# First RMS norm: factor per token applied behind the input projection, x transposed as it lands, first slab in two halves by rows

## The chip, the cores and the metric

The kernel runs on one core of one Trainium2 chip. The metric is the device time of one execution in microseconds. Each profile is of one such execution.

## The reference

Two transformer blocks on 256 tokens of width 1024, in float32. What bears on the change is the head of the first block:

```
xn = x * rsqrt(mean(x * x, axis=-1) + EPS) * attn_norm_g      # one factor per token, one gain per feature
proj = xn @ w_in                                              # mq, mk, mv (softmax attention), gq, gk, gv, gr, gate_lr (gated linear attention)
mq, mk = rope(mq), rope(mk)                                   # cos and sin per token and feature
log_a = log_sigmoid(gate_lr @ w_gate_up + b_gate) / 16
og = gla_attention(gq, gk, gv, log_a)                         # chunked, G = cumsum(log_a)
y_gla = rms_norm(og) * gla_norm_g * silu(gr)
```

After it follow the output projection, a feed-forward with a short convolution, and the second block, which the change leaves alone.

## The kernel before, in words

Every engine has its own program, written out by hand, and engines wait for each other on semaphores. All weights come as 117 slabs of 128 x 2048 floats (1 MB), in the order of the list `STREAM`, through three buffers `raw`. For each slab ScalarE (ACT) writes the rounded high part `hiw` (L616, helper `rnd`) and VectorE (DVE) the rest, `low` = raw - hiw (L1059, helper `res`); both have three buffers too. TensorE (PE) then makes three products per tile of 128 x 128: high by high, high by low, low by high (`three`, L1702 to L1704), 48 of 256 columns for a slab of the input projection. SyncE (SP) issues the next slab when `low` of the slab three before it is made.

The start: PE multiplies zeros `WARM` = 12 times (`keep_clock`, L1634) while x comes in. ACT squares token tile 0 and half of tile 1 (`first_squares`), DVE the other half; the factor of each token comes out of a logarithm and an exponential. DVE multiplies the rows of x by it (L1072), PE turns the 16 tiles (`first_turn`, L1647), ACT makes the high part `xhi` with the gain per feature (L645), DVE the rest `xlo` (L1080). Then PE computes `gg`, the small product for the gates, with `smh` and `sml`; two more products of zeros; the slab `gq` in two halves by columns; `z`, the gates' second product (L1835); the slab `gk`; and then the slabs mq0, mk0, mv0, mq1, mk1, mv1, gv0, gv1, gr0, gr1. Behind slab k stand the score products of the gated attention, one level of block size L after another (`level`; L1862 for most, L1859 for L = 128). The levels 0 and 128 both come behind mq0.

GpSimd (POOL) prepares the levels. It starts on two events, and for the first two levels does four differences and two scalings of 128 x 256, with an exponential of ACT between them:

```
pool.wait_ge(*given_back("gk"))
pool.wait_ge(s("gates_summed"), 1)
for i, L in enumerate(GLA_LEVELS[1:]):
    ...
    pool.tensor_tensor(late, g_late, mid, ALU.subtract)
    pool.tensor_tensor(early, mid, g_early, ALU.subtract).then_inc(s("level_diff"), 1)
    if i:
        scale_level(i - 1)
```

`given_back("gk")` is the moment at which the slab's product has been copied out of PSUM; `gates_summed` comes from DVE's running sums (L1187). PE's level 128 waits for the first `scale_level` (L559, L560), in line with everything behind it. `tok`, `gg`, `z` and so on are leases of PSUM banks: `full` is PE's signal, `given_back` the reader's.

## Time and profile before

| | |
|---|---|
| time, median of 3 runs | 737.99 us (737.91 to 738.71) |
| the profiled execution | 737.9 us, of which the span of the trace is 736.1 us |
| PE busy | 720.2 us (98%) |
| DVE busy, ACT busy, POOL busy | 546.8 us (74%), 380.1 us (52%), 57.2 us (8%) |
| DMA | 129.27 MB, mean 176 GB/s |

Busy shares are means over the whole span. What bounds a stretch is read from who waits in it: from the chain of waits, followed back from the last instruction, and from the timeline.

### The profile page before, as it was taken

The numbers are of one execution on the slowest core, as the hardware profiler recorded it, in microseconds if no ns is written. First come the engines' busy times: TensorE is split into PE (matmuls) and PEld (weight loads), VectorE is DVE, ScalarE is ACT, GpSimd is POOL, SyncE is SP. The second block draws the span as 40 slices with busy tenths as digits, with TensorE's granted clock in tenths as the row PEclk, the third lists the DMA queues.
The fourth block names the chain that finished last, engine by engine and source line by source line (L and its number), as shares of the span: only waits on it lengthen the run. The fifth ranks groups of instructions, "written<-read, shape, count | busy, mean of one in ns | idle before, by whom it ended". The sixth has DMA issues, their size and how long they took to land.

```text
span 736.1 us, 11503 instructions
## 1 busy us (share of the span) xinstructions
PE 720.2 (98%) x4488; PEld 637.9 (87%) x4488; DVE 546.8 (74%) x645; ACT 380.1 (52%) x471; POOL 57.2 (8%) x64
## 2 busy tenths in 40 slices
PE   8999999999999999989999999999999999999998
PEld 8999887888888888778989888999888888888886
DVE  6679847889998889966558857787788666656663
ACT  7635466766555555555564543544457344344341
POOL 1455100000330000011000000000000000000000
PEclk9999999999999999999999999999999999999999
DMA  9835333165555555333543444445535655455431
GB/s 361 321 131 202 115 115 145 71 228 206 209 177 212 181 177 211 127 115 132 215 155 134 168 172 172 172 172 202 198 115 179 222 190 210 171 187 212 173 115 57
DMA packets 18954, 129.27 MB, mean 176 GB/s; under 512 B 2272, under 2 KB 2528, under 8 KB 3680
## 3 DMA queue, kind: packets, MB, share of 16 engines
q1 hardware_dynamic: 18912, 128.68, 48.0%
q8 instruction: 30, 0.49, 0.3%
q14 instruction: 12, 0.10, 0.0%
HBM read 126.57 MB, written 1.05 MB: 173 GB/s over the span
## 4 chain that ended last, share of the span: by engine, by line
PE 90%; DVE 6%; ACT 2%; issue 1%; POOL 0%; DVEq 0%; POOLq 0%; ACTq 0%
PE ps L1726 20%; PE ps L1702 13%; PE ps L1703 13%; PE ps L1704 13%; PE ps L1734 10%; PE ps L1746 7%; PE ps L1748 4%; DVE low L1059 2%; ACT hiw L616 1%; PE ps L1862 1%; PE ps L1634 1%; PE ps L1674 1%; PE ps L1682 1%; PE ps L1675 1%; PE ps L1659 1%
## 5 line engine op out<-in xcount | busy, mean ns | idle before, releaser
L616 ACT ACTIVATE hiw<-raw 128x2048 fp32r<-128x2048 f32 x116 | 222.0, 1915 | 205.8 <-PE ps L1734 97.6
L1059 DVE TENSOR_TENSOR low<-raw,hiw 128x2048 fp32r<-128x2048 f32 x116 | 267.9, 2313 | 80.2 <-ACT hiw L616 79.6
L1726 PE MATMUL ps<-xx,hiw 128*128 128x512 f32 x672 | 159.9, 390 | 0.0
L1726 PEld LDWEIGHTS ps<-xx,hiw 128*128 128x128 f32 x672 | 124.5, 188 | 24.8
L1734 PEld LDWEIGHTS ps<-xx,low 128*128 128x128 f32 x672 | 86.0, 191 | 3.1
L1734 PE MATMUL ps<-xx,low 128*128 128x256 f32 x672 | 87.3, 283 | 0.0
L1702 PE MATMUL ps<-hiw,yhi 128*128 128x512 f32 x208 | 81.7, 393 | 2.0 <-DVE ylo L1363 1.5
L1703 PE MATMUL ps<-low,yhi 128*128 128x512 f32 x208 | 81.2, 390 | 0.0
L1704 PE MATMUL ps<-hiw,ylo 128*128 128x512 f32 x208 | 81.0, 389 | 0.0
L1318 DVE TENSOR_REDUCE arena<-ps 128x512 f32<-128x1024 f32 x42 | 51.3, 1221 | 24.1 <-PE ps L1734 24.0
L1746 PE MATMUL ps<-xx,hiw 128*128 128x512 f32 x256 | 64.8, 395 | 0.9 <-DVE arena L1537 0.9
L1702 PE MATMUL ps<-xx,hiw 128*128 128x256 f32 x224 | 64.3, 287 | 1.0 <-DVE low L1059 1.0
L1703 PE MATMUL ps<-xx,hiw 128*128 128x256 f32 x224 | 63.3, 283 | 0.0
L1704 PE MATMUL ps<-xx,low 128*128 128x256 f32 x224 | 63.3, 283 | 0.0
L1746 PEld LDWEIGHTS ps<-xx,hiw 128*128 128x128 f32 x256 | 46.1, 189 | 10.1 <-DVE arena L1537 1.1
L1702 PEld LDWEIGHTS ps<-hiw,yhi 128*128 128x128 f32 x208 | 39.1, 188 | 10.6 <-DVE ylo L1363 1.9
L1704 PEld LDWEIGHTS ps<-hiw,ylo 128*128 128x128 f32 x208 | 39.1, 188 | 8.3
L1703 PEld LDWEIGHTS ps<-low,yhi 128*128 128x128 f32 x208 | 39.1, 188 | 7.3
L1336 DVE SCALAR_TENSOR_TENSOR arena<-arena,vec 128x255 f32<-128x255 f32 x88 | 40.5, 481 | 5.8 <-ACT arena L863 1.5
L1702 PEld LDWEIGHTS ps<-xx,hiw 128*128 128x128 f32 x224 | 42.9, 192 | 2.0 <-issue 1.7
L1703 PEld LDWEIGHTS ps<-xx,hiw 128*128 128x128 f32 x224 | 42.9, 192 | 0.0
L1704 PEld LDWEIGHTS ps<-xx,low 128*128 128x128 f32 x224 | 42.9, 192 | 0.0
(239 smaller groups left out, 1023.1 us busy)
## 6 DMA issues: line engine op xcount, KB each, us to landing
raw<-in_slabs SPq DMA_DIRECT2D x117, 1024.0 KB, 4.8
vec<-in_vec SPq DMA_DIRECT2D x1, 1258.5 KB, 9.0
cst<-in_cst SPq DMA_DIRECT2D x1, 1220.0 KB, 13.3
h<-in_x SPq DMA_DIRECT2D x2, 512.0 KB, 3.7
arena<-arena SPq DMA_DIRECT2D x16, 64.0 KB, 2.8
out<-h SPq DMA_DIRECT2D x1, 512.0 KB, 2.7
out<-h SPq DMA_DIRECT2D x2, 256.0 KB, 2.0
vec<-in_vec SPq DMA_DIRECT2D x1, 229.0 KB, 4.8
```

What stands on the lines that cost most here:

```text
L616: act.activation(hiw[:, n % SPLIT, :], raw[:, n % RAW, :], ACT.Copy).then_inc(hi_made, 1)
L1059: dve.tensor_tensor(low[:, n % SPLIT, :], raw[:, n % RAW, :], hiw[:, n % SPLIT, :].bitcast(F32), ALU.subtract).then_inc(lo_made, 1)
L1318: dve.tensor_reduce((hid if k == "ffn1" else up)[par][j], wide_hidden(j).rearrange("p c (a b) -> p c b a", a=2), AX_X, ALU.add).then_inc(h ...
L1336: ins = dve.scalar_tensor_tensor(out=dst[:, o:], in0=src[:, 0:T - o], scalar=w, in1=dst[:, o:], op0=ALU.mult, op1=ALU.add)
L1634: pe.matmul(bank(name)[:, 0:P], zeros[:, :], zeros[:, :], start=True, stop=True)
L1702: pe.matmul(o, whi, mhi, start=start, stop=False)
L1703: pe.matmul(o, whi, mlo, start=False, stop=False)
L1704: return pe.matmul(o, wlo, mhi, start=False, stop=stop)
L1726: pe.matmul(banks[:, c, :], hi[:, kt, cc_], xx[:, kt].rearrange("p a b -> p (a b)"), start=kt == 0, stop=False)
L1734: mm = pe.matmul(banks[:, c, 0:T], lo[:, kt, cc_], xhi[:, kt, :], start=False, stop=kt == KT - 1)
L1746: pe.matmul(o, hi[:, kt, cc_], xx[:, kt].rearrange("p a b -> p (a b)"), start=kt == 0, stop=False)
L1748: mm = pe.matmul(o[:, 0:T], lo[:, kt, cc_], xhi[:, kt, :], start=False, stop=kt == KT - 1)
```

## The change

The rows of x are no longer scaled. PE turns x itself, tile 0 as soon as it and the identity have landed, then tile 1. `xhi` and `xlo` hold x times the gain alone. Everything computed from them lacks the factor of its token, which is multiplied in later: where tokens lie on partitions (mv0, mv1, gv0, gv1) by ACT as it copies out of PSUM; where tokens lie in columns (gg, gq, gk, gr0, gr1) by DVE with a tile `token_scale`, which holds the factors along the columns and is made by two small products (`spread_tokens`) inside the slab gq; for mq and mk in the tables of cosine and sine. ACT squares tile 0 first and tile 1 only behind the first slab's rounding. The first slab comes as two transfers, by rows (contraction tiles 0 to 3, then 4 to 7). PE does all its products with the high part first, then `spread_tokens`, then those with the low part; gk goes the same way. The vectors' first part comes in two transfers, the constants' first part ahead of x's tile 1. The warm-up has 8 products of zeros in place of 12, and the two ahead of gq are gone.

```diff
-WARM = 12
+WARM = 8
...
-            for tt in range(TT):
-                sp.dma_start(h[:, tt, :], x_in[tt * P:(tt + 1) * P, :]).then_inc(s(f"x{tt}_in"), 16)
+            sp.dma_start(h[:, 0, :], x_in[0:P, :]).then_inc(s("x0_in"), 16)
             sp.dma_start(cst[:, 0:C_FIRST], cst_in[:, 0:C_FIRST]).then_inc(s("cst_first_in"), 16)
-            sp.dma_start(vec[:, 0:V_FIRST], vec_in[:, 0:V_FIRST]).then_inc(s("vec_first_in"), 16)
-            sp.dma_start(raw[:, 0, :], slabs_in[0]).then_inc(raw_full[0], 16)
+            sp.dma_start(h[:, 1, :], x_in[P:T, :]).then_inc(s("x1_in"), 16)
+            sp.dma_start(vec[:, 0:V_GAINS], vec_in[:, 0:V_GAINS]).then_inc(s("vec_gains_in"), 16)
+            sp.dma_start(row_half(raw[:, 0, :], 0), row_half(slabs_in[0], 0)).then_inc(s("half_in"), 16)
+            sp.dma_start(row_half(raw[:, 0, :], 1), row_half(slabs_in[0], 1)).then_inc(raw_full[0], 16)
+            sp.dma_start(vec[:, V_GAINS:V_FIRST], vec_in[:, V_GAINS:V_FIRST]).then_inc(s("vec_first_in"), 16)
...
-            act.wait_ge(*full("gg"))
-            act.activation(ggT[0:GATE_RANK, :], bank("gg")[0:GATE_RANK, 0:T], ACT.Copy).then_inc(*frees("gg"))
-            evacuate("gq", gqT, scale=SCALE)
+            act.wait_ge(s("vec_first_in"), 16)
             act.wait_ge(*full("z"))
...
             rnd(3)
-            evacuate("gk", gkT)
             rnd(4)
...
-                evacuate(name, DST[name])
+                if name[1] == "v":
+                    act.wait_ge(*full(name))
+                    for tt in range(TT):
+                        ins = act.activation(DST[name][:, tt, :], bank(name)[:, tt * 256:(tt + 1) * 256], ACT.Copy,
+                                             scale=norm_scale(0, tt))
+                    ins.then_inc(*frees(name))
+                elif name[1] != "r":
+                    evacuate(name, DST[name])
...
+            def times_tokens(name, dst, scale=1.0):
+
+                dve.wait_ge(*full(name))
+                n = token_scale.unsqueeze(1).broadcast_to([P, 2, T])
+                dve.scalar_tensor_tensor(out=dst, in0=two(name), scalar=scale, in1=n, op0=ALU.mult,
+                                         op1=ALU.mult).then_inc(*frees(name))
...
+            dve.wait_ge(s("rstd_made"), TT)
+            for tt in range(TT):
+                dve.tensor_scalar(spread[:, tt, :], onesT[:, 0:P], norm_scale(0, tt), None, ALU.mult)\
+                   .then_inc(s("spread_made"), 1)
+            dve.wait_ge(*full("tok"))
+            dve.tensor_copy(token_scale, bank("tok")[:, 0:T]).then_inc(*frees("tok"))
+            dve.wait_ge(*given_back("tok"))
+            dve.wait_ge(*full("gg"))
+            dve.tensor_tensor(ggT[0:GATE_RANK, :], bank("gg")[0:GATE_RANK, 0:T], token_scale[0:GATE_RANK, :],
+                              ALU.mult).then_inc(*frees("gg"))
             res(1)
+            times_tokens("gq", gqT, SCALE)
             res(2)
...
             last.then_inc(s("gates_summed"), 1)
+            times_tokens("gk", gkT)
             res(3)
             dve.wait_ge(s("cst_rest_in"), 16)
             me.step(dve, dve.tensor_reduce(st[:, 34:35], C(C_ROT), AX_X, ALU.add))
-            me.step(dve, dve.tensor_scalar(sin_signed, C(C_SIN, T), st[:, 34:35], -1.0, ALU.mult, ALU.mult))
+            dve.scalar_tensor_tensor(out=sin_signed, in0=C(C_SIN, T), scalar=st[:, 34:35], in1=token_scale,
+                                     op0=ALU.mult, op1=ALU.mult)
+            me.step(dve, dve.tensor_tensor(C(C_COS, T), C(C_COS, T), token_scale, ALU.mult))
...
+                if k >= 10:
+                    times_tokens(IN1[k], grT[:, 2 * (k - 10):2 * (k - 10) + 2, :])
...
                 for tt in range(TT):
+                    pe.wait_ge(s(f"x{tt}_in"), 16)
                     for kt in range(KT):
-                        if kt % 4 == 0:
-                            pe.wait_ge(s("rows_scaled"), 2 * tt + kt // 4 + 1)
                         o = bank(f"n0_{kt // 2}")[:, kt % 2 * T + tt * P:kt % 2 * T + (tt + 1) * P]
-                        mm = pe.transpose(o, hn[0][:, tt, kt * P:(kt + 1) * P], ident)
+                        mm = pe.transpose(o, h[:, tt, kt * P:(kt + 1) * P], ident)
...
+            def first_slab(o, n):
+
                 hi, lo = slab_views(n, KT)
+                for half, high_made in enumerate(((s("half_hi"), 1), (hi_made, 1))):
+                    pe.wait_ge(*high_made)
+                    for c in range(2):
+                        for kt in range(half * KT // 2, (half + 1) * KT // 2):
+                            for m in (xhi, xlo):
+                                pe.matmul(o[:, c * T:(c + 1) * T], hi[:, kt, c * P:(c + 1) * P], m[:, kt, :],
+                                          start=half == 0 and c == 0 and kt == 0 and m is xhi, stop=False)
+                spread_tokens()
...
             take_bank(pe, "gq")
-            keep_clock("gq", 2)
-            pe.wait_ge(s("half_lo"), 1)
-            feature_half(bank("gq"), AT[("in1", "gq")], 0)
-            pe.wait_ge(lo_made, 1)
-            feature_half(bank("gq"), AT[("in1", "gq")], 1).then_inc(*fills("gq"))
+            first_slab(bank("gq"), AT[("in1", "gq")]).then_inc(*fills("gq"))
```

**The order on PE at the start.** Before, the 16 turns (L1647) stand behind 12 products of zeros and behind the scaled rows (`rows_scaled`, DVE's L1072):

```order
L1634 MATMUL ps<-zeros 128x128 [waits zeros_made]
L1634 MATMUL ps<-zeros 128x128 x11
L1647 MATMUL ps<-cst,arena 128x128 [waits rows_scaled,cst_first_in]
L1647 MATMUL ps<-cst,arena 128x128 x3
L1647 MATMUL ps<-cst,arena 128x128 [waits rows_scaled]
```

Of the change, where the turns are L1657, the products of gq L1784 (high) and L1791 (low), and the two small products L1800:

```order
L1645 MATMUL ps<-zeros 128x128 x7
L1657 MATMUL ps<-cst,h 128x128 [waits x0_in,cst_first_in]
L1657 MATMUL ps<-cst,h 128x128 x7
L1657 MATMUL ps<-cst,h 128x128 [waits x1_in]
```

```order
L1784 MATMUL ps<-xx,hiw 128x256 [waits half_hi]
L1784 MATMUL ps<-xx,hiw 128x256 x15
L1784 MATMUL ps<-xx,hiw 128x256 [waits hi_made]
L1784 MATMUL ps<-xx,hiw 128x256 x15
L1800 MATMUL ps<-cst,arena 128x128 [waits spread_made] x2
L1791 MATMUL ps<-xx,low 128x256 [waits half_lo]
```

The turns wait for transfers alone, and the two small products stand between the high and the low products of the first slab.

**The order on DVE from the gates' running sums to the slab mq0.** Before (L1187 are the sums, L1059 the low parts of slabs 3 and 4, L1192 the sine table):

```order
L1187 SCALAR_TENSOR_TENSOR arena<-arena 128x256
L1059 TENSOR_TENSOR low<-raw,hiw 128x2048 [waits hi_made]
L1191 TENSOR_REDUCE st<-cst 128x1 [waits cst_rest_in]
L1192 TENSOR_SCALAR arena<-cst,st 128x256 [waits dve_step]
L1059 TENSOR_TENSOR low<-raw,hiw 128x2048 [waits hi_made,dve_step]
```

Of the change (L1159 is `times_tokens` of gk, waiting for PE's bank; L1199 and L1201 are the sine and the cosine table):

```order
L1193 SCALAR_TENSOR_TENSOR arena<-arena 128x256
L1159 SCALAR_TENSOR_TENSOR arena<-ps,arena 128x512 [waits bank_full1]
L1059 TENSOR_TENSOR low<-raw,hiw 128x2048 [waits hi_made]
L1198 TENSOR_REDUCE st<-cst 128x1 [waits cst_rest_in]
L1199 SCALAR_TENSOR_TENSOR arena<-cst,st,arena 128x256 [waits dve_step]
L1201 TENSOR_TENSOR cst<-cst,arena 128x256
L1059 TENSOR_TENSOR low<-raw,hiw 128x2048 [waits hi_made,dve_step]
```

Copying gk out of PSUM has moved from ACT to DVE, ahead of the low part of slab 3, and one more instruction stands between the low parts of slabs 3 and 4.

## Rows read from the trace of the kernel before

**Rows 1.** The page: the chain that ended last, share of the span by engine.
```profile
PE 90%; DVE 6%; ACT 2%; issue 1%; POOL 0%; DVEq 0%; POOLq 0%; ACTq 0%
```

**Rows 2.** The chain of waits, 0 to 10 us: start, length, what.
```profile
0.98 5.49 PE ps L1634 x24
...
8.00 0.85 ACT xx L645 x2
```

**Rows 3.** Timeline to 27 us: start us, us, engine line op out<-in [idle before <-releaser].
```profile
4.06 1.06 ACT L625 ACTIVATE arena<-h 128x1024 f32<-128x1024 f32 x1 [2.05 <-DMA h<-in_x]
...
5.29 0.69 DVE L1066 CUSTOM_DVE_ANT_0 arena<-h 128x512 f32<-128x512 f32 x1 [5.29 <-DMA h<-in_x]
...
10.87 2.06 ACT L692 ACTIVATE hiw<-raw 128x1024 fp32r<-128x1024 f32 x2
...
19.27 1.13 PE L1835 MATMUL ps<-arena,vec 16*128 16x256 f32 x4
...
26.38 0.60 ACT L680 ACTIVATE arena<-ps 128x512 f32<-128x512 f32 x1 [1.30 <-PE ps L1704]
```

**Rows 4.** Lines L1634 (to 6.5 us, and at 13 us) and L1647: ns min/median/max.
```profile
L1634 PE MATMUL ps<-zeros x21: 421/421/421, 1.8 to 6.1; 128*128 128x128 f32 x21
...
L1634 PE MATMUL ps<-zeros x3: 271/274/275, 13.0 to 13.2; 128*128 128x128 f32 x3
...
L1647 PE MATMUL ps<-cst,arena x9: 272/273/329, 7.3 to 8.3; 128*128 128x128 f32 x9
```

**Rows 5.** SP's issues, and DMA issues to 20 us (KB each, median us to landing).
```profile
1.64 0.43 SPq L490 DMA_DIRECT2D cst<-in_cst  x1
2.11 0.43 SPq L491 DMA_DIRECT2D vec<-in_vec  x1
...
vec<-in_vec SPq DMA_DIRECT2D x1, 229.0 KB, 4.8
cst<-in_cst SPq DMA_DIRECT2D x1, 66.0 KB, 4.1
```

**Rows 6.** Timeline of DVE and POOL, 25 to 35 us.
```profile
25.22 2.27 DVE L1059 TENSOR_TENSOR low<-raw,hiw 128x2048 fp32r<-128x2048 f32 x1
...
27.72 0.39 DVE L1192 TENSOR_SCALAR arena<-cst,st 128x256 f32<-128x256 f32 x1
28.88 2.43 DVE L1059 TENSOR_TENSOR low<-raw,hiw 128x2048 fp32r<-128x2048 f32 x1 [0.77 <-ACT hiw L616]
33.22 1.29 DVE L1202 TENSOR_TENSOR arena<-ps,cst 128x512 f32<-128x512 f32 x2 [1.91 <-PE ps L1862]
...
27.05 0.91 POOL L577 TENSOR_TENSOR arena<-arena 128x256 f32<-128x256 f32 x1 [23.94 <-ACT arena L680]
...
28.55 0.62 POOL L577 TENSOR_TENSOR arena<-arena 128x256 f32<-128x256 f32 x1
29.13 2.66 POOL L578 TENSOR_TENSOR arena<-arena 128x256 f32<-128x256 f32 x1
31.75 0.73 POOL L559 TENSOR_TENSOR arena<-arena 128x256 f32<-128x256 f32 x1
32.44 0.73 POOL L560 TENSOR_TENSOR arena<-arena 128x256 f32<-128x256 f32 x1
```

**Rows 7.** Level 128 on PE: its row, and its wait (total us, times, longest).
```profile
33.22 0.72 PE L1859 MATMUL ps<-arena 64*128 64x128 f32 x8
...
PEld ps L1859 <- POOL arena L560: 0.2, 1, 0.2
```

**Rows 8.** Timeline of DVE and POOL, 43 to 48 us.
```profile
43.95 1.18 POOL L560 TENSOR_TENSOR arena<-arena 128x256 f32<-128x256 f32 x1
...
44.45 2.82 DVE L1059 TENSOR_TENSOR low<-raw,hiw 128x2048 fp32r<-128x2048 f32 x1
```

**Rows 9.** PE's waits over the whole span, the longest single one.
```profile
PE ps L1885 <- DVE arena L1245: 1.6, 1, 1.6
```

**Rows 10.** Timeline of DVE near slab gr0.
```profile
100.46 2.29 DVE L1059 TENSOR_TENSOR low<-raw,hiw 128x2048 fp32r<-128x2048 f32 x1 [6.12 <-ACT hiw L616]
```

More of the change, by code:

```diff
@@ L92 @@
 V_W = _at
+V_GAINS = V_LAY["small"][1]
 V_FIRST = V_LAY["wup"][1]
@@ L402, in build @@
         ggT = piece(5120, 256)
+        spread, token_scale = piece(12288, TT, P), piece(4608, T)
         gqT, gkT, G = (piece(5376 + 512 * j, 2, T) for j in range(3))
@@ L466, in pv_done, with row_half @@
             return full(f"mo{hh // 2}" if hh < 8 else f"fo{(hh - 8) // 2}")
-        def column_half(t, c):
-            return t.rearrange("p (k c) -> p k c", k=KT)[:, :, c * P:(c + 1) * P]
+        def row_half(t, half):
+            return t[:, half * SLAB // 2:(half + 1) * SLAB // 2]
         def level_halves(t, i):
@@ L682, in _ @@
             tables("natural_log_exp_and_others")
[L683 to L688 removed]
+            first_sum(0)
+            act.wait_ge(s("vec_gains_in"), 16)
             first_turned()
+            act.wait_ge(s("half_in"), 16)
+            act.activation(row_half(hiw[:, 0, :], 0), row_half(raw[:, 0, :], 0), ACT.Copy).then_inc(s("half_hi"), 1)
             act.wait_ge(raw_full[0], 16)
[L691 to L693 removed]
+            act.activation(row_half(hiw[:, 0, :], 1), row_half(raw[:, 0, :], 1), ACT.Copy).then_inc(hi_made, 1)
+            first_sum(1)
             rnd(1)
             rnd(2)
[L697 to L699 removed]
+            act.wait_ge(s("vec_first_in"), 16)
             act.wait_ge(*full("z"))
@@ L766, in _ @@
             DST = {"mq0": qpre[0], "mk0": qpre[1], "mq1": qpre[0], "mk1": qpre[1], "mv0": mv[:, :, 0, :],
-                   "mv1": mv[:, :, 1, :], "gv0": gv[:, :, 0, :], "gv1": gv[:, :, 1, :], "gr0": grT[:, 0:2, :],
-                   "gr1": grT[:, 2:4, :]}
+                   "mv1": mv[:, :, 1, :], "gv0": gv[:, :, 0, :], "gv1": gv[:, :, 1, :]}
             ropes = 0
@@ L1172, in _ @@
             first_turned()
-            dve.wait_ge(s("half_hi"), 1)
-            dve.tensor_tensor(column_half(low[:, 0, :], 0), column_half(raw[:, 0, :], 0),
-                              column_half(hiw[:, 0, :], 0).bitcast(F32), ALU.subtract).then_inc(s("half_lo"), 1)
-            dve.wait_ge(hi_made, 1)
-            dve.tensor_tensor(column_half(low[:, 0, :], 1), column_half(raw[:, 0, :], 1),
-                              column_half(hiw[:, 0, :], 1).bitcast(F32), ALU.subtract).then_inc(lo_made, 1)
-            dve.memset(onesT, 1.0).then_inc(s("ones_made"), 1)
+            for half, (high, low_half) in enumerate((((s("half_hi"), 1), (s("half_lo"), 1)), ((hi_made, 1), (lo_made, 1)))):
+                dve.wait_ge(*high)
+                dve.tensor_tensor(row_half(low[:, 0, :], half), row_half(raw[:, 0, :], half),
+                                  row_half(hiw[:, 0, :], half).bitcast(F32), ALU.subtract).then_inc(*low_half)
+            dve.wait_ge(s("ones_made"), 1)
+            dve.wait_ge(s("rstd_made"), TT)
[8 more added lines that the diff above has]
+                              ALU.mult).then_inc(*frees("gg"))
             res(1)
+            times_tokens("gq", gqT, SCALE)
             res(2)
             dve.wait_ge(s("z_ln"), 1)
-            dve.wait_ge(s("ones_made"), 1)
             me.step(dve, dve.scalar_tensor_tensor(out=zb, in0=zb, scalar=0.0, in1=za, op0=ALU.min, op1=ALU.subtract))
@@ L1764, in feature_major_late, with spread_tokens @@
                 return mm
-            def feature_half(o, n, c):
+            def first_slab(o, n):
                 hi, lo = slab_views(n, KT)
-                cc_ = slice(c * P, (c + 1) * P)
-                for kt in range(KT):
-                    mm = three(o[:, c * T:(c + 1) * T], hi[:, kt, cc_], lo[:, kt, cc_], xhi[:, kt, :], xlo[:, kt, :],
-                               kt == 0, kt == KT - 1)
-                return mm
+                for half, high_made in enumerate(((s("half_hi"), 1), (hi_made, 1))):
[6 more added lines that the diff above has]
+                spread_tokens()
+                for half, low_made in enumerate(((s("half_lo"), 1), (lo_made, 1))):
+                    pe.wait_ge(*low_made)
+                    for c in range(2):
+                        for kt in range(half * KT // 2, (half + 1) * KT // 2):
+                            mm = pe.matmul(o[:, c * T:(c + 1) * T], lo[:, kt, c * P:(c + 1) * P], xhi[:, kt, :],
+                                           start=False, stop=half == 1 and c == 1 and kt == KT - 1)
+                return mm
+            def spread_tokens():
+                take_bank(pe, "tok")
+                for tt in range(TT):
+                    pe.wait_ge(s("spread_made"), tt + 1)
+                    mm = pe.matmul(bank("tok")[:, tt * P:(tt + 1) * P], spread[:, tt, :], ident, start=True, stop=True)
+                mm.then_inc(*fills("tok"))
             def token_major(o, n, middle=None):
```

52 lines of the change are left out of this document (17 added, 35 removed).

## The prediction

> **What bounds the kernel now.** I read the chain of waits first. PE holds 90% of it, DVE 6%, ACT 2% [rows 1]: PE runs nearly without a gap, so a microsecond counts only if it moves PE's next instruction. Then I read the chain's first 10 us. The reader is to see that PE's products of zeros carry it to about 6.5 us, and that `xhi` starts at 8.0 [rows 2]; everything on PE hangs on that start. The timeline gives the fixed points behind it: the first slab's rounding at 10.87, `z` on PE at 19.27, and the copy of gk out of PSUM at 26.38, which says that PE ended gk at 26.35 [rows 3]. Last I read the two engines that are not in the chain, DVE and POOL, around the first levels [rows 6], because the change reorders DVE exactly there. PE reached level 128 at 33.2 and waited 0.2 us for POOL's L560 [rows 7]. That small wait is the hinge of this forecast: POOL's preparation of level 128 was already level with PE.
>
> **The start, step by step.** Removed: the scaling of the rows (DVE, L1072) and the wait for both factors. The new gate for the turns is landing plus warm-up. The 24 halves of 12 products of zeros took 5.49 us [rows 2], or 0.22 to 0.23 us each, so 16 of them end at 0.98 + 3.6 = 4.6 us. x's tile 0 had landed when ACT started at 4.06, tile 1 when DVE started at 5.29 [rows 3]. The constants, queued behind both, landed at 1.64 + 4.1 = 5.7, and the vectors at 2.11 + 4.8 = 6.9 [rows 5]. In the new order the constants go second. I take 4.5 for them (0.45 behind x's tile 0, as they were behind tile 1), 5.7 for tile 1 (the same bytes as before the constants' old landing), and 6.3 for the gains (half of the vectors' old 1.2 us). The bounds for the constants are 4.1 and 5.7.
>
> The turns then run from 4.6. PE's clock matters here. The products of zeros took 421 ns each until 6.1 us and 271 to 275 ns at 13 us, and the turns from 6.5 us on took 272 ns [rows 4]: PE was at 1.2 GHz for the whole warm-up and at 2.4 GHz behind it, having multiplied without a stop since 0.98. Nine turns begin between 7.3 and 8.3, so one costs about 0.11 us at the high level [rows 4], and I take twice that, 0.21, at the low one. Eight turns of tile 0 end at 6.3, two of tile 1 are out by 6.5 to 6.6, and the result is there 0.2 to 0.3 us later: `xhi` starts at 6.8 in place of 8.0. **The lead is 1.2 us.** It is at most 1.7, when PE is at the high level from the start of the turns and the gains' landing at 6.3 is the gate; it is at least 0.5, when the constants land at 5.7 and tile 0 is turned after that.
>
> Between `xhi` and `z` the changed steps balance. From `z` at 19.27 to gk's copy at 26.38 PE did `z` (1.1 us) and 48 products [rows 3], some 0.12 us each; counted back, 48 of them and 0.4 us for two products of zeros put the end of gg at 12.9 before and 11.7 now. ACT's rounding of the first slab keeps its distance of 2.87 us from `xhi` (8.00 to 10.87 [rows 2, 3]), so the halves are rounded at 10.8 and 11.8; PE needs the first at 11.7 and the second, 16 products on, at 13.6. The two products of zeros ahead of gq go, and `spread_tokens` brings two of the same shape: nothing. The factors: ACT squares tile 1 behind the rounding (1.06 us for tile 0 [rows 3], and under 1 us for logarithm and exponential), is done by 13.7, and PE asks for the spread at 15.5. ACT's rounding of slab 1 is 0.5 us later than before and PE asks for it at 19.1. Those costs are all nothing as long as PE is that late; if the cover went, each would cost its excess alone. So `z` starts at 18.1, and gk ends at 26.4 - 1.2 = 25.2.
>
> Later additions: mv and gv leave PSUM in two instructions instead of one (some 0.15 us more of ACT, which waits for PE's banks around them), gr0 and gr1 move to DVE, which was idle 6.1 us there [rows 10]. Nothing.
>
> **What the lead runs into.** POOL may start on the levels when gk is out of PSUM. Before, from 26.4 on: DVE's low part of slab 3 had begun at 25.22, so POOL's first difference at 27.05 was held only for its tail (0.91 us where an undisturbed one takes 0.62). The low part of slab 4 then started at 28.88, and POOL's fourth difference took 2.66 us, 2.05 more than its own length; when DVE was done, POOL went on with L559 at 31.75 and L560 at 32.44, each about 0.7 [rows 6]. It holds the other way too: the low part took 2.82 us beside POOL's L560, which took 1.18, against 2.27 alone [rows 6, 8]. So the two engines exclude each other in such instructions, and take turns.
>
> Of the change, DVE has to wait for gk before it makes the low part of slab 3, since `times_tokens` of gk now stands ahead. POOL is released by that same copy, while DVE goes straight on into the low part. POOL now meets the whole of it and not its tail. From the end of gk, in us:
>
> - copy of gk on DVE, half of the pair of equal size at 33.22 [rows 6]: 0.65
> - low part of slab 3, POOL held: 2.1
> - four differences of POOL: 2.4
> - the sine and the cosine table, two inputs from SBUF each, where the sine had one (0.39 us, which held nobody): 0.3 each, 0.6
> - low part of slab 4, which is ready before the fourth difference: 2.1
> - the two scalings: 1.4
>
> That is 9.25 us, so L560 ends at 25.2 + 9.25 = 34.45, where before it ended at 33.17. PE would reach level 128 at 33.2 - 1.2 = 32.0 and stands 2.5 us. Level 128 starts 1.25 us later than before. If the two tables hold nobody, it is 8.65 us and 0.65 later. ACT's exponential and its rounding of slab 4 (1.9 us from 25.2) lie inside. Queued behind level 128 on PE is everything: mk0, level 64, the other slabs. On ACT the exponential for the next level, the copy of mq0 and the rounding of slab 5 stand behind POOL's fourth difference, so they move with PE's delay. I find no wait on PE after this that ends at a transfer or at another event not itself set off by PE, so the 1.25 us reach the end.
>
> **The rule that speaks against the change.** The Trainium skill, page "SBUF — State Buffer", section "Who interferes with whom", says that a VectorE instruction with two SBUF inputs and a GpSimd instruction that reads SBUF hold a shared port for the whole of each instruction. By that rule both tables belong in the list, which gives the larger sum, 739.15; without the rule the rows leave 738.55 open. The 2.66 us of [rows 6] agree with it.
>
> **The sum.** The profiled execution took 737.9 us, its span 736.1, so 1.8 lie around it; it is 0.1 under the median of the runs, 737.99. 737.9 + 1.25 = 739.15. I forecast 739.1 us.
>
> **The rivals.**
>
> 1. *The lead survives*: POOL gets through between DVE's instructions. If it does its four differences in one go after the low part of slab 3, L560 ends at 25.2 + 0.65 + 2.1 + 2.4 + 1.4 = 31.75, ahead of PE's 32.0, and the time is 737.9 - 1.2 = 736.7 (736.2 to 737.4 over the lead's bounds). For it: DVE pauses between reduction and tables, and the low part of slab 4 might come late. Against it: at 28.88 DVE came up while POOL was in its third difference, and DVE went first [rows 6]. A milder form, in which one of the low parts falls outside POOL's work, gives 25.2 + 7.15 = 32.35, 0.85 earlier than before: 737.05.
>
> 2. *The start gains nothing, and the stall comes all the same*: slower. The place is the turns; the price is the lead. If the constants land at 5.7 or PE is still at 1.2 GHz when gg begins, the lead is 0, gk ends at 26.4 and L560 at 35.65, which makes 740.35. It decides from a lead under 0.9, where the end passes 0.2% over the median. For it: with 8 products of zeros there is a possible gap before the turns, which was none before. Against it: the turns take the place of the zeros, so PE multiplies on from 4.6 to about 7.5. The Trainium skill, page "TensorE: Matmul & The Clock Gate", section "What's actually happening", says that the moment of the rise differs between runs of one kernel. No run here shows that yet; it would widen the lead on both sides.
>
> 3. *PE falls back to 1.2 GHz in the 2.5 us stall*: its longest wait before was 1.6 us, with no fall [rows 9]. Each product of 256 columns would then cost about double for a while; I price it at 1 to 3 us on top, 740 to 742, and hold it unlikely, 3 in 100, counted with the second.
>
> **How the numbers follow.** What a measurement of this kernel can tell from no change is about 0.2%, 1.5 us: 736.5 to 739.5. The stall with most of the lead gained: 0.54, on its own 738.1 to 739.85 (lead 1.2 give or take, tables counted or not), of which 0.14 lies above 739.5. The lead survives: 0.24, half of it below 736.5 since the lead's upper bound is 1.7, and possible small gains at the tail of gg come on top. The milder form: 0.09, all within. No lead, or a fall of the clock: 0.13, nearly all above. That makes faster 0.13, same 0.60, slower 0.27. The range leaves out about 0.1 at either end: 736.4 to 740.0.
>
> **What the profile after would show.** The lead: `xhi` on ACT at 6.8 (6.3 to 7.5), `z` on PE at 18.1, gk full at 25.2. The stall: a DVE low part starting at about 25.8 with POOL's first L-difference behind it at over 2.5 us; another POOL difference of over 2.5 us up to 33; L560 ending at 34.4; and on PE a wait of about 2.5 us at level 128, for POOL. If PE's wait there is under 0.5 us, the forecast is wrong and the first rival holds. If `xhi` starts after 7.5, the second does. If the sine and cosine rows are no longer than 0.4 us and POOL's beside them no longer than 0.7, the tables held nobody. Wrong in another way would be a wait for raw slabs on ACT before 25 us: the low parts of slabs 1 and 2 are made some 2 us later, and with them the issues of slabs 4 and 5.

## The result, and the profile after

The changed kernel took 741.85 us (median of 5 runs, 739.0 to 742.42), the kernel before 737.99 us (5 runs, 737.73 to 738.71). The ratio is 1.0044, interval 1.0028 to 1.006: it is slower by 3.9 us, more than the 1.25 us of the forecast, and above the range's 740.0. The profiled execution took 742.42 us, 4.5 more than the one before.

The page of the profile after, the chain by engine, answers to [rows 1]; POOL and DMA have each gained a share, PE has lost two points:

```profile
PE 88%; DVE 6%; ACT 2%; POOL 2%; issue 1%; DMA 1%; SPq 0%; DVEq 0%; POOLq 0%; ACTq 0%
```

The chain of waits over the first 12 us (start, length, what), for [rows 2]. The chain comes from a transfer now, that of the gains, where it came from PE's products of zeros before:

```profile
2.11 5.49 DMA vec<-in_vec
7.62 0.85 ACT xx L645 x2
...
8.49 0.89 DVE xx L1067 x2
...
9.52 0.36 PE ps L1712
```

The timeline of the same stretch and of PE around z and the levels, for [rows 3, 7]. L1657 are the turns, L1859 is `z`, L1888 is level 0 and, at 44.34, level 64, L1885 is level 128; the bracket is idle time before the row and what ended it:

```profile
4.24 1.06 ACT L630 ACTIVATE arena<-h 128x1024 f32<-128x1024 f32 x1 [2.23 <-DMA h<-in_x]
...
4.56 1.91 PE L1657 MATMUL ps<-cst,h 128*128 128x128 f32 x8
...
6.75 1.10 PE L1657 MATMUL ps<-cst,h 128*128 128x128 f32 x8 [0.28 <-DMA h<-in_x]
7.62 3.03 ACT L645 ACTIVATE xx<-ps,vec 128x256 fp32r<-128x256 f32 x8 [1.67 <-DMA vec<-in_vec]
...
9.52 0.36 PE L1712 MATMUL ps<-xx,smh 128*128 128x256 f32 x1 [1.67 <-DVE xx L1067]
...
20.24 1.13 PE L1859 MATMUL ps<-arena,vec 16*128 16x256 f32 x4
...
32.99 1.16 PE L1888 MATMUL ps<-arena 64*128 64x128 f32 x16
36.27 0.72 PE L1885 MATMUL ps<-arena 64*128 64x128 f32 x8 [2.12 <-POOL arena L565]
44.34 1.16 PE L1888 MATMUL ps<-arena 64*128 64x128 f32 x16
```

Tile 1 was turned at 6.75, when it landed, and `xhi` began at 7.62, when the gains had landed, not at 8.00 [rows 2]: a lead of 0.4 us. That lead is one execution's. Five more kernels of the experiments below (e1, e2, e7, e9, e13) issue x's tile 1 and the gains in the same places; in their profiled executions `xhi` began at 8.06, 7.86, 7.68, 8.09 and 8.72. Of the six, the changed kernel's is the earliest, and three are later than before. Yet in the execution shown here `z` began at 20.24, 1.0 us later than before. At level 128, where PE had waited 0.2 us [rows 7], it stood 2.12 us for POOL, and level 128 began at 36.27 in place of 33.22.

DVE and POOL of the changed kernel from 26 us on answer to [rows 6] (L1159 copies gk, L1059 the low parts of slabs 3 and 4, L1199 and L1201 the tables):

```profile
27.34 0.69 DVE L1159 SCALAR_TENSOR_TENSOR arena<-ps,arena 128x512 f32<-128x512 f32 x1 [1.01 <-PE ps L1772]
27.95 2.28 DVE L1059 TENSOR_TENSOR low<-raw,hiw 128x2048 fp32r<-128x2048 f32 x1
...
30.46 0.53 DVE L1199 SCALAR_TENSOR_TENSOR arena<-cst,st,arena 128x256 f32<-128x256 f32 x1
30.91 0.83 DVE L1201 TENSOR_TENSOR cst<-cst,arena 128x256 f32<-128x256 f32 x1
31.77 2.60 DVE L1059 TENSOR_TENSOR low<-raw,hiw 128x2048 fp32r<-128x2048 f32 x1
...
28.11 2.59 POOL L582 TENSOR_TENSOR arena<-arena 128x256 f32<-128x256 f32 x1 [25.00 <-DVE arena L1159]
30.67 0.79 POOL L583 TENSOR_TENSOR arena<-arena 128x256 f32<-128x256 f32 x1
31.42 0.80 POOL L582 TENSOR_TENSOR arena<-arena 128x256 f32<-128x256 f32 x1
32.19 2.66 POOL L583 TENSOR_TENSOR arena<-arena 128x256 f32<-128x256 f32 x1
34.81 0.73 POOL L564 TENSOR_TENSOR arena<-arena 128x256 f32<-128x256 f32 x1
35.49 0.72 POOL L565 TENSOR_TENSOR arena<-arena 128x256 f32<-128x256 f32 x1
```

Two of POOL's differences took 2.59 and 2.66 us, each beside one of DVE's low parts, as forecast. From the start of gk's copy to the end of L565 it is 36.21 - 27.34 = 8.9 us; the prediction said 9.25.

What it did not say shows in the table by windows (each engine's busy time; the number behind POOL's is the granted clock):

```profile
10.20:13.20 3.00, 3.00 (x16) 3.00 (x15) 3.00 (x6) 3.00 (x5) 0.00 (x0) 0.50 1.01 427
37.50:40.50 3.00, 3.00 (x16) 3.00 (x15) 2.63 (x1) 1.47 (x4) 3.00 (x3) 0.50 0.65 202
40.80:43.80 3.00, 3.00 (x27) 3.00 (x27) 0.00 (x0) 0.00 (x0) 0.94 (x2) 1.00 0.67 270
```

Twice TensorE was granted half its speed, 1.2 GHz in place of 2.4: from about 10.05 us, behind the 1.67 us stop ahead of gg, and from about 37.35 us, behind the 2.12 us stop at level 128. In 3 us it began 16 products in place of 27. The durations of one line's products at either level (ns, min/median/max):

```profile
L1713 PE MATMUL ps<-xx,hiw x5: 415/415/415, 37.6 to 40.1; 128*128 128x256 f32 x5
...
L1713 PE MATMUL ps<-xx,hiw x8: 280/283/283, 40.8 to 43.3; 128*128 128x256 f32 x8
```

The falls can be priced by distances that hold no other difference. From `xhi` to `z` it was 19.27 - 8.00 = 11.27 us before and 20.24 - 7.62 = 12.62 after: the first fall cost 1.35. From level 128 to the next level on PE it was 6.59 before (the next level began at 39.81, row below) and 44.34 - 36.27 = 8.07 after: the second cost 1.5. Before:

```profile
39.81 1.16 PE L1862 MATMUL ps<-arena 64*128 64x128 f32 x16
```

All together: lead -0.38, first fall +1.35, gk's copy to level 128 8.93 in place of 6.84 = +2.09, second fall +1.48, sum 4.54. The next level began 4.53 later, and DVE's low part near gr0 still stands 4.53 behind the 100.46 of [rows 10], at 104.99. Nothing is lost or won in between:

```profile
104.99 2.29 DVE L1059 TENSOR_TENSOR low<-raw,hiw 128x2048 fp32r<-128x2048 f32 x1 [3.71 <-ACT hiw L621]
```

The five runs fit: with a mean granted clock of 1.0 it took 739.0 us, with 0.998 740.92, with 0.995 741.85, 742.02 and 742.42. The mean clock of a run has a blind spot, though. In the kernel before, the products of zeros took 421 ns each until 6.1 us [rows 4], which is the low level, and the view shows a granted clock of 1.00 there (the number third from the end):

```profile
5.00:6.00 1.00, 1.00 (x6) 1.00 (x6) 0.70 (x3) 0.94 (x5) 0.00 (x0) 1.00 1.05 335
```

So it counts the falls, and not the time before the first rise. Nor is the kernel before free of falls: it ran 73 times beside the experiments, and three of those runs had a clock of 0.998 and took 739.5 to 739.94 us.

### The profile page after: what moved, and what is told of

Read it like the earlier page. It is cut to its first block, busy times and chain, and to the rows that moved or that the text cites. A ratio compares the mean times of both kernels' runs of the same rounds, so it can differ in the third digit from the quotient of the medians.

```text
span 740.6 us, 11495 instructions
## 1 busy us (share of the span) xinstructions
PE 722.1 (97%) x4480; PEld 639.8 (86%) x4480; DVE 549.6 (74%) x650; ACT 378.8 (51%) x468; POOL 59.0 (8%) x64
## 4 chain that ended last, share of the span: by engine, by line
PE 88%; DVE 6%; ACT 2%; POOL 2%; issue 1%; DMA 1%; SPq 0%; DVEq 0%; POOLq 0%; ACTq 0%
PE ps L1736 20%; PE ps L1712 13%; PE ps L1713 12%; PE ps L1714 12%; PE ps L1744 10%; PE ps L1756 7%; PE ps L1758 4%; DVE low L1059 2%; PE ps L1767 1%; ACT hiw L621 1%; PE ps L1684 1%; DMA vec<-in_vec 1%; PE ps L1888 1%; PE ps L1692 1%; PE ps L1685 1%
## 5 line engine op out<-in xcount | busy, mean ns | idle before, releaser
L1059 DVE TENSOR_TENSOR low<-raw,hiw 128x2048 fp32r<-128x2048 f32 x116 | 268.1, 2315 | 78.7 <-ACT hiw L621 78.3
L1736 PEld LDWEIGHTS ps<-xx,hiw 128*128 128x128 f32 x672 | 124.5, 188 | 24.8
L1744 PEld LDWEIGHTS ps<-xx,low 128*128 128x128 f32 x672 | 86.0, 191 | 3.1
L1744 PE MATMUL ps<-xx,low 128*128 128x256 f32 x672 | 87.3, 283 | 0.0
L1712 PE MATMUL ps<-xx,hiw 128*128 128x256 f32 x192 | 55.9, 291 | 1.0 <-DVE low L1059 1.0
L1714 PE MATMUL ps<-xx,low 128*128 128x256 f32 x192 | 55.0, 286 | 0.0
L1713 PE MATMUL ps<-xx,hiw 128*128 128x256 f32 x192 | 55.0, 286 | 0.0
L1756 PEld LDWEIGHTS ps<-xx,hiw 128*128 128x128 f32 x256 | 46.1, 189 | 10.1 <-DVE arena L1548 1.1
L1712 PEld LDWEIGHTS ps<-xx,hiw 128*128 128x128 f32 x192 | 37.5, 195 | 1.7 <-issue 1.4
L1713 PEld LDWEIGHTS ps<-xx,hiw 128*128 128x128 f32 x192 | 37.6, 196 | 0.0
L1714 PEld LDWEIGHTS ps<-xx,low 128*128 128x128 f32 x192 | 37.5, 195 | 0.0
```

The costliest lines, as they stand in the source:

```text
L1059: dve.tensor_tensor(low[:, n % SPLIT, :], raw[:, n % RAW, :], hiw[:, n % SPLIT, :].bitcast(F32), ALU.subtract).then_inc(lo_made, 1)
L1712: pe.matmul(o, whi, mhi, start=start, stop=False)
L1713: pe.matmul(o, whi, mlo, start=False, stop=False)
L1714: return pe.matmul(o, wlo, mhi, start=False, stop=stop)
L1736: pe.matmul(banks[:, c, :], hi[:, kt, cc_], xx[:, kt].rearrange("p a b -> p (a b)"), start=kt == 0, stop=False)
L1744: mm = pe.matmul(banks[:, c, 0:T], lo[:, kt, cc_], xhi[:, kt, :], start=False, stop=kt == KT - 1)
```

## The experiments

My theory at this point: POOL's chain behind gk explains some 2 us, two falls of the clock 1.4 to 1.5 each, and late landings ate the lead. The rival: the stops and falls are bystanders, and the transposed x or the first slab by halves costs time elsewhere. In the expectations, "least run" is the fastest run. Each ratio is taken against runs of the kernel before made beside it, with medians of 737.87 to 737.96 us.

**e1_fill_turn**: turns of zeros fill the hole ahead of gg.

```diff
             first_turn()
+            take_bank(pe, "gg")
+            keep_clock("gg", 6)
             small_product("gg", slice(0, 128), 0)
```

> The changed kernel with 6 products of zeros between the turns and gg, where PE stood 1.7 us. Theory 'clock': PE's stop before gg is what let the clock fall at 10.05 us, so with the zeros gg runs at 2.4 GHz, z starts at about 18.9 in place of 20.2, the stall at level 128 stays (about 2.1 us) and may still bring the second fall: profile 1.4 us shorter, 741.0 or less. Rival 'phase': the clock falls at a moment of its own, whatever PE does; then gg still holds products of 415 ns in some runs and the median stays at 741.5 to 742.

Measured: 741.03 us (739.36 to 742.58, 6 runs), ratio 1.0037 [1.0025, 1.0049]. The profiled execution (741.46) has no fall at 10 us: `xhi` to `z` is 11.27 again (8.06 to 19.33). Tile 1 came later than in the changed kernel (turned at 7.38 behind a wait of 1.26), so the lead was gone. The stop at level 128 stayed and the second fall with it, so the second doesn't need the first.

**e2_fill_128**: eight zeros fill the stop at level 128.

```diff
                     i = GLA_LEVELS.index(L) - 1
+                    if L == 128:
+                        take_bank(pe, "lev128_0")
+                        keep_clock("lev128_0", 8)
                     pe.wait_ge(s("level_scaled"), i + 1)
```

> The changed kernel with 8 products of zeros ahead of level 128, in the 2.1 us in which PE waited for POOL. Theory 'clock': mk0 then runs at 2.4 GHz (products of 283 ns, none of 415 behind level 128), which is 1.5 us less: 740.3 where the first fall stays. The wait itself stays filled, so nothing else is gained. Rival 'phase': the second fall comes anyway and the time stays near 742.

Measured: 739.76 us (739.27 to 742.02, 6 runs), ratio 1.0033 [1.0021, 1.0045]; four runs at 739.27 to 739.79 with clock 1.0, two at 741.59 and 742.02 with 0.995. PE of the profiled execution (739.73):

```profile
31.86 1.16 PE L1891 MATMUL ps<-arena 64*128 64x128 f32 x16
32.96 2.05 PE L1645 MATMUL ps<-zeros 128*128 128x128 f32 x16
35.16 0.72 PE L1888 MATMUL ps<-arena 64*128 64x128 f32 x8 [0.15 <-POOL arena L565]
41.74 1.16 PE L1891 MATMUL ps<-arena 64*128 64x128 f32 x16
```

Level 128 still waits for POOL, but the next level comes 6.58 us later, not 8.07. The products of zeros don't shorten the stall; in this execution they take away the fall behind it. The two runs at 741.59 and 742.02 have no trace; where they lost their clock isn't known. The other traces help: of eight profiled executions in which PE stood here for 1.8 us or more with nothing in the hole, seven have a fall (the changed kernel, e1, e3, e5, e7, e12, e13), which begins between the end of the stop and 1.1 us after it and moves with it, and one has none (e11). So the second fall comes with the stop, not at a moment of its own.

**e3_before_gk_dve**: the kernel before, with gk alone moved from ACT to DVE.

```diff
-            evacuate("gk", gkT)
...
             last.then_inc(s("gates_summed"), 1)
+            dve.wait_ge(*full("gk"))
+            dve.tensor_copy(gkT, two("gk")).then_inc(*frees("gk"))
             res(3)
```

> The kernel before with one thing of the change: gk is copied out of PSUM by DVE, ahead of the low part of slab 3, no factor, same tables. Theory 'order on DVE': POOL's first difference meets the whole low part (2.6 us), L560 ends at 26.35 + 0.65 + 2.1 + 2.4 + 2.1 + 1.4 = 35.0, PE waits 1.7 us at level 128: 1.6 to 1.8 us slower, and up to 1.5 more where the clock falls in that wait: 739.6 to 741.2. Rival 'the added table instruction and the lost lead do it': then this kernel stays within 0.4 us of before.

Measured: 741.14 us (739.56 to 741.19, 5 runs), ratio 1.0037 [1.0024, 1.005]. Nothing of the start is changed, and `z` stands at 19.29. Four runs at 741.12 to 741.19 have clock 0.997, one at 739.56 has 1.0. POOL and the clock behind level 128:

```profile
27.16 2.59 POOL L577 TENSOR_TENSOR arena<-arena 128x256 f32<-128x256 f32 x1 [24.05 <-DVE arena L1189]
...
30.34 2.66 POOL L577 TENSOR_TENSOR arena<-arena 128x256 f32<-128x256 f32 x1
```
```profile
35.00 0.71 PE L1860 MATMUL ps<-arena 64*128 64x128 f32 x8 [1.80 <-POOL arena L560]
```
```profile
36.00:39.20 3.20, 3.20 (x17) 3.20 (x17) 2.62 (x1) 1.70 (x4) 3.20 (x3) 0.50 0.51 172
```

The run without a fall is 1.6 us over the 737.96 of the kernel before, the others are another 1.6 over that. So one moved copy costs 1.6 us by the stall and 1.6 more by the fall behind it, 3.2 together, beside the change's 3.9.

**e4_before_warm8**: the kernel before with `WARM = 8`.

> The kernel before with 8 products of zeros in place of 12, nothing else. PE stops from 4.7 to 6.5 us, before the turns. Theory 'clock': the rise comes later or the fall comes behind the turns in most runs; the turns and gg then hold products at 1.2 GHz, 0.5 to 2 us slower. Rival 'the number of warm-up products is free': within 0.3 us of before.

Measured: 739.37 us (737.91 to 741.65, 12 runs), ratio 1.0021 [1.0011, 1.003]. The hole ahead of the turns was 2.03 us, and the runs scatter: three are level with before, three have clocks of 0.995 to 0.998 (739.73 to 739.96), and six have 1.0 and still 738.88 to 741.65. So the shorter warm-up has a price of its own in nine of twelve runs. What those six lost I can't say: the profiled execution is one that lost nothing (737.95). A later first rise is possible, since the mean clock doesn't count it; no run here shows it.

**e5_gains_first**: the gains are issued ahead of x's tile 1.

```diff
+            sp.dma_start(vec[:, 0:V_GAINS], vec_in[:, 0:V_GAINS]).then_inc(s("vec_gains_in"), 16)
             sp.dma_start(h[:, 1, :], x_in[P:T, :]).then_inc(s("x1_in"), 16)
-            sp.dma_start(vec[:, 0:V_GAINS], vec_in[:, 0:V_GAINS]).then_inc(s("vec_gains_in"), 16)
```

> The changed kernel with the gains (and the small weights) issued ahead of x's tile 1. In the changed kernel xhi waited for them until 7.6 us. Theory 'order of transfers': they land by 6.3, xhi then starts with tile 1's turns, which wait for a landing near 7: 0.3 to 0.6 us gained at xhi, none of it lost later, but the falls of the clock stay: about 741.5, least run 738.5. Rival 'the queue as a whole is late': tile 1 slides by as much as the gains come forward, and xhi starts at 7.6 again: no difference.

Measured: 743.83 us (742.22 to 744.54, 5 runs), ratio 1.0074 [1.0061, 1.0087]. The gains landed 3.0 us after their issue instead of 5.5, and tile 1 was later still:

```profile
4.66 0.34 DVE L1166 CAST smh<-vec 128x128 fp32r<-128x128 f32 x2 [3.53 <-DMA vec<-in_vec]
...
7.69 1.10 PE L1657 MATMUL ps<-cst,h 128*128 128x128 f32 x8 [1.22 <-DMA h<-in_x]
```

`xhi` began at 8.23, later than before the change. That the gains went in front at tile 1's expense isn't shown: tile 1 landed at 7.6 here, and between 6.7 and 7.9 in the six kernels that have only the constants ahead of it. Nor is the late start what made this kernel the slowest of all. Its profiled execution (744.54) has both falls and a third, behind a stop that the kernel before has as well, the one of [rows 9], at 79.58 there:

```profile
84.72 0.52 PE L1911 MATMUL ps<-cst,arena 128*128 128x128 f32 x3 [1.55 <-DVE arena L1254]
```
```profile
86.00:87.00 1.00, 1.00 (x8) 0.67 (x5) 1.00 (x3) 0.27 (x1) 0.00 (x0) 0.50 0.97 401
```

All its runs have clocks of 0.993 to 0.995. Why this kernel falls more often stays open.

**e7_one_slab**: the first slab in one transfer again.

```diff
-            sp.dma_start(row_half(raw[:, 0, :], 0), row_half(slabs_in[0], 0)).then_inc(s("half_in"), 16)
-            sp.dma_start(row_half(raw[:, 0, :], 1), row_half(slabs_in[0], 1)).then_inc(raw_full[0], 16)
+            sp.dma_start(raw[:, 0, :], slabs_in[0]).then_inc(raw_full[0], 16)
...
-            act.wait_ge(s("half_in"), 16)
+            act.wait_ge(raw_full[0], 16)
```

> The changed kernel with its first slab in one transfer again (rows of 8 KB), ACT still rounding it in two halves. Theory 'rows of 4 KB': the two halves' shorter rows slowed and mixed with x's tile 1 and the gains, so tile 1 lands near 5.7 and the gains near 6.5, xhi starts at about 6.8: 0.8 us gained, least run 738.3. Rival 'the first bytes are slow whatever stands behind them': tile 1 at 6.7 to 7.4 and the gains at 7.6 as before; the slab's rounding is not later either, since ACT comes to it at 10.5 only.

Measured: 741.07 us (739.48 to 743.4, 6 runs), ratio 1.0043 [1.003, 1.0056]. Tile 1 was turned at 7.15 behind a wait of 1.24, the gains took 5.5 us to land, `xhi` began at 7.68, all within what the kernels with halves show. The halves are not what delays the landings.

**e9_res4_late**: the low part of slab 4 moves behind `level_scores(0)` on DVE.

```diff
-                if k < 11:
+                if k == 2:
+                    res(4)
+                if 1 < k < 11:
                     res(k + 3)
```

> The changed kernel with the low part of slab 4 moved behind the scores of level 0 on DVE. Theory 'POOL held by the low part': POOL's fourth difference takes 0.6 to 0.8 us in place of 2.66, L565 ends 1.9 us earlier, PE's wait at level 128 falls from 2.1 to about 0.2 and the second fall of the clock goes with it: 1.9 to 3.4 us less, least run near 737.2. What may come in its place is a wait at level 64, since POOL's scaling for it then meets two low parts: up to 1.3 us of the gain. Rival 'POOL is slow by itself there': the wait stays near 2 us.

Measured: 740.65 us (738.4 to 741.68, 11 runs), ratio 1.0031 [1.0021, 1.004]. The stop at level 128 is gone (34.47, no wait), and a smaller one stands one level on, since two low parts now meet level 64's work:

```profile
35.90 2.66 POOL L583 TENSOR_TENSOR arena<-arena 128x256 f32<-128x256 f32 x1
38.52 2.78 POOL L564 TENSOR_TENSOR arena<-arena 128x256 f32<-128x256 f32 x1
```

PE waited 0.9 us there. The fastest run is 1.2 us over the 737.2 that I expected of it. The profiled run (740.03) has a fall left, at 0.50 from 9.5 us, inside the unfilled hole of 1.34 us ahead of gg; nine of the eleven runs have a mean clock of 0.998 or less, the two at 738.4 have 1.0.

**e10_mended**: e9's order, e1's six zeros, e5's gains first, and the tables and the low part of slab 1 moved ahead on DVE.

> The changed kernel with four mendings: 6 products of zeros behind the turns, gains ahead of x's tile 1, on DVE the low part of slab 1 ahead of the copy of token_scale and the two tables ahead of the gates' sums, and the low part of slab 4 behind the scores of level 0. By the theory of clock, port and transfers: lead of 0.4 to 1 us kept, no wait for POOL at level 128, no falls: 737.0 to 737.6, faster than before by 0.4 to 1. If a wait at level 64 appears: 738 to 738.5.

Measured: 738.73 us (738.14 to 740.61, 11 runs), ratio 1.0013 [1.0004, 1.0021], a little above the 738 to 738.5 expected for a wait at level 64. Ten of eleven runs have clock 1.0. What is left is the 0.9 at level 64 and a late start: tile 1 came at 7.87, `xhi` at 8.41, `z` at 19.98, with 0.3 us more between the last two than before and a wait of 0.23 for DVE in it. With the tables out of POOL's way, its second and third difference took 0.61 and 0.62 us, where they took 0.79 and 0.80 in the changed kernel.

**e11_x_first**: tile 1 is issued ahead of the constants, and `WARM = 12`.

```diff
+            sp.dma_start(h[:, 1, :], x_in[P:T, :]).then_inc(s("x1_in"), 16)
             sp.dma_start(cst[:, 0:C_FIRST], cst_in[:, 0:C_FIRST]).then_inc(s("cst_first_in"), 16)
-            sp.dma_start(h[:, 1, :], x_in[P:T, :]).then_inc(s("x1_in"), 16)
```

> x's tile 1 is issued ahead of the constants, and two more products of zeros warm TensorE. If tile 1 and the gains land late because short-rowed transfers are issued ahead of them, tile 1 lands near 5.3 us as before the change, xhi is there between 7.2 and 7.7, and there is no fall of the clock ahead of gg. The stop of 2.1 us at level 128 stays and with it the fall behind it in most runs: 739 to 741. If the arrival of x is slow whatever is ahead of it, tile 1 is turned after 6.8 again and the time stays at 741 to 742.

Measured: 739.89 us (739.32 to 745.3, 12 runs), ratio 1.0034 [1.0021, 1.0047]. All 16 turns run without a wait for x, `xhi` begins at 7.69, and `z` 11.26 us later; the gains, 5.6 us from issue to landing, are the gate:

```profile
6.27 1.91 PE L1657 MATMUL ps<-cst,h 128*128 128x128 f32 x16
...
7.69 3.03 ACT L645 ACTIVATE xx<-ps,vec 128x256 fp32r<-128x256 f32 x8 [1.78 <-DMA vec<-in_vec]
```

The profiled run (739.56) has no fall at all, though PE stood 2.12 us at level 128: a stop of this length need not bring one. Four of the twelve runs have clocks of 0.993 to 0.998 and took 740.53 to 745.3 us; the fall that I expected in most runs came in a third of them. Its level 128 begins at 34.98, 1.76 after the 33.22 of [rows 7], and its time is 1.66 over the 737.9 before. This is the forecast's mechanism with nothing added.

**e12_three_early** and **e13_three_only**: slab 3's rounding (ACT) and low part (DVE) move ahead of the gates and gk, to leave POOL only slab 4's to meet; in e12 on top of e11's transfers, `WARM = 10` and three zeros ahead of gg. Both also move the two tables ahead of the gates' sums and slab 1's low part ahead of the copy of `token_scale`, which the expectations leave out.

```diff
+            rnd(3)
             act.wait_ge(s("vec_first_in"), 16)
             act.wait_ge(*full("z"))
...
-            rnd(3)
...
             res(2)
+            res(3)
+            tables_of_tokens()
...
             times_tokens("gk", gkT)
-            res(3)
```

> Tile 1 first, three more turns to fill the hole ahead of gg, and the sums of tiles 1 and 2 behind the factors and slab 3's rounding: the rounding of slab 3 runs on ScalarE ahead of z's bias copies and its difference right behind slab 2's, so that GpSimd has only the low part of slab 4 left beside VectorE's copies. If the 4.5 us are the chain on GpSimd plus two falls of the clock, there is no stop over 0.5 us at level 128, no fall, and the time is 737.0 to 738.4, level with the kernel before. If something else behind z costs time, it stays at 739 or above.

> Only slab 3's rounding and difference are moved up (ScalarE ahead of z's bias copies, VectorE right behind slab 2's). The stop at level 128 goes or shrinks under 0.5 us, and the fall behind it goes; the lead stays 0.4 and the stop of 1.7 us ahead of gg stays, with a fall there in most runs: median 738.5 to 739.7, least run near 737.7. If the first fall caused the second, or the stall comes from elsewhere, the median stays over 740.5.

Measured: 741.66 us (741.22 to 742.6, 5 runs), ratio 1.005 [1.0037, 1.0063], and 741.42 us (740.41 to 743.8, 5 runs), ratio 1.0045 [1.0032, 1.0058]. Both of my expectations fell. ACT of e12:

```profile
22.79 1.91 ACT L621 ACTIVATE hiw<-raw 128x2048 fp32r<-128x2048 f32 x1 [5.04 <-DMA raw<-in_slabs]
24.61 0.82 ACT L698 ACTIVATE arena<-ps,vec 128x256 f32<-128x256 f32 x2
```

Slab 3 has not landed before 22.8 us. In front of the gates it holds up everything behind it on ACT and DVE. On DVE its low part ran from 24.73 and the tables from 26.94 to 28.1, and the gates' sums only then: gk was copied at 30.03, and PE stood 3.90 us at level 128. In e13 gk was copied at 31.25 and PE stood 2.15 us there; tile 1 had also come at 7.94, 2.35 us after PE was ready for it, with a fall of the clock right behind. How much of either loss is slab 3's and how much the tables', the two runs don't separate. The move was made against an order of landing that I had not read.

**e14_low_parts_apart**: e11's transfers, `WARM = 10`, three zeros ahead of gg, e9's place for slab 4, and slab 5's low part waits until POOL has scaled level 64.

```diff
-                if k < 11:
+                if k == 2:
+                    res(4)
+                if k == 2:
+                    dve.wait_ge(s("level_scaled"), 2)
+                if 1 < k < 11:
                     res(k + 3)
```

> Tile 1 ahead of the constants, three more turns ahead of gg, and VectorE's low parts kept apart from GpSimd's levels: slab 4's stands behind level_scores(0) and slab 5's waits until level 64 is scaled. If the loss is the late arrival, the meetings of VectorE's copies with GpSimd's chain, and the clock that falls behind PE's stops, then z's product comes before 18.8 us, level 128 has no wait, level 64's is under 0.4 us, the clock stays up, and the time is 736.6 to 737.8: level with the kernel before or under it. If slab 5's low part comes too late for its products, a wait for it stands near 42 us and the time is 738 or more; if the transposed x costs something else behind 50 us, it stays over 738 with no wait there.

Measured: 737.37 us (736.82 to 740.93, 11 runs) beside 737.92 (737.73 to 739.5, 15 runs), ratio 0.9995 [0.9984, 1.0005]. Ten of the eleven runs lie between 736.82 and 737.95, all eleven have clock 1.0 (what the one at 740.93 lost isn't known). POOL, and PE's waits from 9 to 60 us:

```profile
30.75 0.61 POOL L583 TENSOR_TENSOR arena<-arena 128x256 f32<-128x256 f32 x1
...
34.22 2.66 POOL L583 TENSOR_TENSOR arena<-arena 128x256 f32<-128x256 f32 x1
36.84 0.73 POOL L564 TENSOR_TENSOR arena<-arena 128x256 f32<-128x256 f32 x1
```
```profile
PE ps L1716 <- DVE xx L1067: 0.7, 1, 0.7
```

Each level now meets one low part. `xhi` at 7.54 and `z` at 18.80 are 0.46 and 0.47 ahead of before, level 128 at 32.79 is 0.43 ahead, and the profiled time is 0.5 shorter. The small lead reaches the end. The interval still contains no change, so this version is level with the kernel before, not shown to be faster. It takes away the late landing of tile 1, the second low part in one level's preparation and the falls together, and with them the whole 3.9 us: what the rest of the change can cost is little, since the interval ends 0.05% (0.4 us) above the kernel before. The price of the three does not come from this run, since it changes them all at once, but from the rows of e1, e2, e3 and e11.

## Why the prediction was wrong

- **The landings: wrong, and they took the lead.** "I take 4.5 for them, ... 5.7 for tile 1 ..., and 6.3 for the gains." Measured: about 4.4, 6.74 and 7.6. Tile 1's 5.7 assumed the same bytes arrive at the same time whatever is ahead of them. With the constants ahead of it tile 1 came a microsecond later than that, and in the five kernels like it between 7.1 and 7.9. Issued ahead of the constants (e11, e12, e14) it landed at 5.3 to 5.5, as before the change, and PE had no wait for it. The gains were not gained on by halving the vectors: 5.5 us from issue, where the whole had taken 4.8 [rows 5]. The lead was 0.38 instead of 1.2, and under the lower bound of 0.5. That is 0.8 us; and as 0.38 is the best of six executions, the usual lead was about none. By its own sign, "If `xhi` starts after 7.5, the second does", the second rival held, which it priced at 740.35 without a lead.
- **`xhi` to `z`: right.** "The changed steps balance": 11.27 us before, 11.26 in e11 and e14, 11.27 in e1, with gk's copy another 7.1 behind.
- **POOL's chain: right.** 8.9 us against 9.25. The tables stretched two differences to 0.79 and 0.80, together 0.35 us and not 0.6. Both tables held POOL somewhat, 0.53 and 0.83 us long themselves. By the Trainium skill, page "SBUF — State Buffer", section "Who interferes with whom", they should meet POOL; the traces agree, by e10, where the differences beside no table took 0.61 and 0.62. The stop was 2.12 us, not 2.5. e3 has it without the rest of the change, e9 moves it, e14 removes it.
- **The falls of the clock: the step that failed.** "I price it at 1 to 3 us on top, 740 to 742, and hold it unlikely, 3 in 100." The price was right (1.35 and 1.48); the chance was not. Behind the stall four of e3's five runs fell. 3 in 100 is about what the kernel before shows without any such stall, three runs of 73. And the prediction put a fall only behind the 2.5 us stall. It never asked what the gap ahead of gg would do, where PE had waited 1.3 us before and waited 1.7 now. Its reason was one execution, with a 1.6 us wait and no fall [rows 9]. That says little of a longer wait or of one behind a short warm-up, and not even enough of this one: in e5 the same wait has a fall behind it.

The sum redone: forecast 739.15, lead 0.82 smaller, POOL's chain 0.38 shorter, is 739.6. The changed kernel's fastest run took 739.0, e11's profiled one 739.56, e2's fast four 739.3 to 739.8. So without falls the mechanism gives the time within a few tenths. The two falls, 2.83 us, make it 742.4, the profiled run. Without them the time would have come out inside the stated range, near its upper end of 740.0. Between "a gap is worth its own length" and the result stands the clock.

What stays open: why one stop brings a fall and another of the same length doesn't (2.12 us in e11 without, in the changed kernel with); why six runs of e4 lost 0.9 to 3.7 us at a mean clock of 1.0; and why tile 1 lands at 6.7 us in one execution and at 7.9 in another with the same transfers ahead. The orders tried show only that the constants ahead of it delay it, and not the halves of the slab.

## What to carry to other kernels

Where PE is the bound, price a new stall twice: its length, and the fall of the clock that may stand behind it, which here cost about 1.5 us behind a stall of 1.8 to 2.1. Zeros in the hole took away the second part in the profiled executions of e1 and e2, and never the first. Before an instruction that uses both inputs from SBUF is moved on DVE, look at what POOL does in those microseconds; a meeting costs POOL the rest of DVE's instruction, and two low parts in one level's preparation were too many where one was free. And before a load's consumer is moved up, read when the load lands, in more than one execution.

## What the runs showed of the hardware

- A product of 256 columns took 415 ns at a granted clock of 0.5 (1.2 GHz) and 283 at 1.0 (2.4 GHz), and began every 0.21 us instead of every 0.12. Falls of the clock came beside stops of PE from 1.34 us (e9) to 3.90 us (e12), and a length alone doesn't settle it: the profiled execution of e7 had a stop of 1.34 us ahead of gg and no fall there, e4's one of 2.03 us and e11's one of 2.12 us, both without.
- The rise at the start differs between kernels that are the same on PE up to it. Tile 0's eight turns began at 4.54 to 4.56 in eight of them, and took from 1.04 us (e13) over 1.56 (e1) to 1.92 (e5). The Trainium skill, page "TensorE: Matmul & The Clock Gate", section "What's actually happening", says that the moment of the rise differs from run to run; the traces agree.
- x's 512 KB tile 1 landed at 5.3 to 5.5 us with only tile 0 ahead of it (before, e11, e12, e14), and at 6.7 to 7.9 with the 66 KB of the constants between (six executions), though it was issued only 0.46 us later. The gains, 100 KB, took 5.5 to 6.1 us to land from behind it in those six, and 3.0 and 3.9 when issued ahead of it (e5, e10).
